# Index key, decay, beta and index weights in one tile of products, with the key rotated while the convolutions run

## The reference

```python
h = rms_norm(x, norm_g)
proj = jnp.einsum('btd,de->bte', h, w_in)
(qa, ka, va, za, ba, aa, ub, zb, qc, kc, vc, zc, iq, ik, iw, gates) = split_columns(proj)
# delta net: qa, ka, va through a convolution over 4 positions and silu; beta and decay per head
beta = jax.nn.sigmoid(ba)                       # 4 columns
g = -jnp.exp(a_log) * jax.nn.softplus(aa + dt_bias)   # 4 columns
# sparse attention: an indexer chooses the keys
qi = apply_rope(iq.reshape(b, t, 4, 64), cos_i, sin_i)
ki = apply_rope(ik.reshape(b, t, 1, 64), cos_i, sin_i)[:, :, 0]   # one key of 64 columns for 4 heads
wi = iw * (IDX_HEADS ** -0.5 * IDX_DIM ** -0.5)  # 4 columns
dots = jnp.einsum('bqhd,bsd->bqhs', qi_b, ki)
score = jnp.einsum('bqh,bqhs->bqs', wi_b, jax.nn.relu(dots))
_, idx = lax.top_k(score, topk)
```

## Time and profile before

| | |
|---|---|
| median of 3 runs | 1982.15 us (1980.84 to 1982.24) |
| the profiled execution, as timed | 1981.93 us |
| its span, first to last instruction | 1980.1 us |
| PE busy | 1967.1 us, 99% |
| DVE, ACT, POOL busy | 52%, 45%, 43% |
| granted TensorE clock | 1.00 over the span |

### The profile page before, as it was taken

One profiled execution on the slowest core, in us unless ns is written; L12 is line 12 of the kernel. 1 busy time (PEld: TensorE's weight loads), 2 busy tenths in 40 slices (PEclk: granted clock), 3 DMA queues, 4 the chain that ended last, 5 costly groups with the idle time before them and its releaser, 6 DMA issues.

```text
span 1980.1 us, 24451 instructions
## 1 busy us (share of the span) xinstructions
PE 1967.1 (99%) x9420; PEld 1561.4 (79%) x9420; DVE 1022.2 (52%) x1872; ACT 889.3 (45%) x1373; POOL 853.8 (43%) x646
## 2 busy tenths in 40 slices
PE   9999999999999999999999999999999999999999
PEld 6878878777788878787877788677777888888887
DVE  5657755555745568666365658476444346201210
ACT  6455553334345555543343355586455334322321
POOL 5545432433355444333434455455222455444443
PEclk9999999999999999999999999999999999999999
DMA  5334542423534235522424546322111322332332
GB/s 199 119 116 133 133 135 79 161 75 122 188 117 144 97 109 154 162 88 84 150 75 144 182 149 170 125 83 86 54 44 43 128 96 96 102 99 92 100 113 69
DMA packets 94995, 228.52 MB, mean 115 GB/s; under 512 B 29880, under 2 KB 32952, under 8 KB 93568
## 3 DMA queue, kind: packets, MB, share of 16 engines
q1 hardware_dynamic: 93408, 224.34, 35.6%
q10 hardware_dynamic: 1472, 2.62, 0.4%
HBM read 195.06 MB, written 24.64 MB: 111 GB/s over the span
## 4 chain that ended last, share of the span: by engine, by line
PE 85%; DVE 7%; ACT 2%; DMA 2%; SPq 1%; issue 1%; POOL 1%; ACTq 0%; DVEq 0%
PE bank L442 83%; PE bank L445 2%; SPq L371 1%; DVE ER L376 1%; DVE kv L376 1%; ACT lt L428 1%; DVE lt L386 1%; DVE scs L401 1%; DMA kv<-blocks 1%; DVE m8s L398 0%; DVE tmp L376 0%; POOL wl L376 0%; ACT L420 0%; DVE tmp L386 0%; ACT wh L431 0%
## 5 line engine op out<-in xcount | busy, mean ns | idle before, releaser
L376 POOL TENSOR_TENSOR wl<-st,wh 128x512 fp32r<-128x512 f32 x606 | 808.6, 1357 | 1049.3 <-ACT wh L431 1049.3
L442 PE MATMUL bank<-hh,wh 128*128 128x512 f32 x1632 | 658.9, 404 | 2.2 <-POOL hl L376 0.7
L442 PE MATMUL bank<-hh,wl 128*128 128x512 f32 x1632 | 636.1, 390 | 0.0
L442 PE MATMUL bank<-hl,wh 128*128 128x512 f32 x1632 | 635.6, 390 | 0.0
L431 ACT ACTIVATE wh<-st 128x1024 fp32r<-128x1024 f32 (+1 forms) x304 | 318.8, 1049 | 235.5 <-PE bank L442 188.3
L442 PEld LDWEIGHTS bank<-hh,wh 128*128 128x128 f32 x1632 | 306.4, 188 | 93.3 <-issue 25.8
L442 PEld LDWEIGHTS bank<-hl,wh 128*128 128x128 f32 x1632 | 306.6, 188 | 67.4 <-issue 6.9
L442 PEld LDWEIGHTS bank<-hh,wl 128*128 128x128 f32 x1632 | 306.3, 188 | 65.4
L376 DVE TENSOR_TENSOR xt<-xt,bank 128x512 f32<-128x512 f32 x40 | 27.4, 686 | 235.6 <-PE bank L442 235.6
L428 ACT ACTIVATE tmp<-bank 128x512 f32<-128x512 f32 x70 | 41.7, 596 | 157.7 <-PE bank L442 151.0
L442 PE MATMUL bank<-fh,wh 128*128 128x512 f32 x256 | 99.6, 389 | 0.0
(11 more groups left out here) (340 smaller groups left out, 2907.8 us busy)
## 6 DMA issues: line engine op xcount, KB each, us to landing
st<-units SPq DMA_DIRECT2D x302, 512.0 KB, 3.5
gates<-tmp SPq DMA_DIRECT2D x48, 256.0 KB, 2.8
gt<-gates SPq DMA_DIRECT2D x48, 256.0 KB, 3.7
pad<-tmp SPq DMA_DIRECT2D x32, 128.0 KB, 2.7
qk<-tmp SPq DMA_DIRECT2D x16, 256.0 KB, 4.3
x_scratch<-xt SPq DMA_DIRECT2D x2, 2048.0 KB, 8.7
xt<-x_scratch SPq DMA_DIRECT2D x2, 2048.0 KB, 8.4
ph<-phi SPq DMA_DIRECT2D x8, 512.0 KB, 4.7
```

Of the source, the lines that this page charges most:

```text
L376: return NOTHING if self.e is None else self.e.tensor_tensor(out, a, b, op)
L442: return NOTHING if self.e is None else self.e.matmul(out, lhsT, rhs, start=start, stop=stop, skip_group_check=share)
```

## The change

The 64 columns of the index key move into the unit of "small", at rows 64 to 127; the index weights move to rows 4 to 7. The tile ("ik") and its unit go, in both layers. ACT copies rows 64 to 127 of bank 4 out beside convolution 0; SP waits for that copy (after feeding two more units, and in layer 0 the load of the tables) and issues five DMAs: four make the swapped halves for both halves of the partitions, one doubles the key itself. DVE rotates it (three instructions) beside convolution 5. The index weights are written by DVE to rows 64 to 71 of `L.rw` (eight rows, of which 68 to 71 are used). ACT's gates 4 and 5 wait for the last convolution in place of `ki`. `proj` has 30 tiles for 31 on every engine; `delta`, `select` and their rates stay. The diff, cut to its core:

```diff
@@ plan, pack_units
-        out += [("p", l, 5128), ("p", l, 5256), ("ik", l)]
+        out += [("p", l, 5128), ("p", l, 5256)]
...
-            for c0, at in ((2048, 0), (2052, 32), (5448, 64)):
-                u[:, :, at:at + 4] = kmajor(w[:, c0:c0 + 4]).reshape(128, 8, 4)
+            for c0, at, m in ((2048, 0, 4), (5448, 4, 4), (2052, 32, 4), (5384, 64, 64)):
+                u[:, :, at:at + m] = kmajor(w[:, c0:c0 + m]).reshape(128, 8, m)
@@ build
+        L.ik, L.iks = [L.lT[:, c, :, :].rearrange("p a b -> p (a b)") for c in range(2)]
@@ tensor_program, proj
-                yield tile(("ik", l), 2, ("ik", l), g), idle(1)
@@ scalar_program, front1 and proj
                     ac.wait_ge(*done("small", l))
+                    ac.cp(L.ik[64:128, :], banks[4][64:128, :]).then_inc(*sig("ik", l))
...
-            def index_k():
-                ac.wait_ge(*done("ik", l))
-                ac.cp(tmp[2][:], banks[2][:]).then_inc(*sig("free2", "ik", l))
-                yield
...
-                ac.wait_ge(*(at("ki", l) if j < 6 else at(f"spill{gate_at(j)}", "gate", l, j - 2)))
+                ac.wait_ge(*(at("conv_v", l, 11, 4) if j < 6 else at(f"spill{gate_at(j)}", "gate", l, j - 2)))
...
-                yield tile(("ik", l)), index_k()
@@ vector_program, front1, proj and delta
-                    dv.ts(L.rw[R2, :], banks[4][R2, :], 1.0 / 16.0, ALU.mult).then_inc(*sig("free4", "small", l))
+                    dv.ts(L.rw[64:72, :], banks[4][0:8, :], 1.0 / 16.0, ALU.mult).then_inc(*sig("free4", "small", l))
+                if c == 5:
+                    dv.wait_ge(*at("tab", "A"))
+                    index(L.ki[:], L.ik, L.iks, at("swapik", l, 4), "ki", l)
...
-            def index_k():
-                yield
-                index(L.ki[:], tmp[2], tmp[3][:], at("swap2", l, 96), "ki", l)
...
-                yield idle(1), index_k()
...
-            dv.cp(L.wi[:], bv[:, :, 64:68]).then_inc(*sig("free4", "tp", l))
+            dv.cp(L.wi[:], bv[:, :, 68:72]).then_inc(*sig("free4", "tp", l))
@@ pool_program
-                for _ in range(31):
+                for _ in range(30):
@@ sync_program, proj and the layer's main line
-            def index_k():
-                sp.wait_ge(*at("free2", "ik", l))
-                swap(tmp[3], tmp[2], 32, "swap2", l)
-                yield
...
-                yield tile(), index_k()
...
             take(2)
             if l == 0:
                 sp.dma(tabs[:, 0:apack.n], tabA).then_inc(*dma("tab", "A"))
+
+            sp.wait_ge(*at("ik", l))
+            for f in range(2):
+                sp.dma(L.iks[64 * f:64 * f + 32, :], L.ik[96:128, :]).then_inc(*dma("swapik", l, 2 * f))
+                sp.dma(L.iks[64 * f + 32:64 * f + 64, :], L.ik[64:96, :]).then_inc(*dma("swapik", l, 2 * f + 1))
+            sp.dma(L.ik[0:64, :], L.ik[64:128, :]).then_inc(*dma("swapik", l, 4))
             take(10)
```

More of the change, by code:

```diff
@@ L2010, in rope, with index @@
             dv.tt(out, out, s1, ALU.add).then_inc(*sig(name, *key))
+        def index(out, x, xs, swapped, name, *key):
+            dv.wait_ge(*swapped)
+            dv.tt(out, x[:], TA("cosI"), ALU.mult).then_inc(*sig("rope", name, *key, 0))
+            dv.tt(xs, xs, TA("sinI"), ALU.mult).then_inc(*sig("rope", name, *key, 1))
+            dv.wait_ge(*at("rope", name, *key, 1))
+            dv.tt(out, out, xs, ALU.add).then_inc(*sig(name, *key))
         def front1(l):
@@ L2049, in proj @@
             dv.wait_ge(*at("tab", "A"))
[L2051 to L2056, removed]
             def index_q(c):
```

## The result

The changed kernel takes **1994.9 us** (median of 6 runs, 1992.9 to 2004.9) beside 1982.1 for the kernel before: ratio 1.0072, 95% interval 1.0051 to 1.0092. It is slower by 13 us; 1973.0 was forecast, so it missed the forecast by 22.

What follows compares the result with a forecast made beforehand. PE's work was taken to bound the kernel, DVE's inversion a close second limit. Layer 0: -5.44 - 0.9 + 1.4 - 1.3 + 1.2 = -5.0; layer 1: -4.0; together -9.1 from 1981.93, forecast 1973.0 us, range 1969.0 to 1977.5.

Steps and rivals of the forecast that it cites:

- A tile's worth: One tile of `proj` removed per layer saves PE 5.44 us, 10.9 us over two layers.
- 1, front1 at nothing: In front1, ACT's copy, DVE's 2.0 us rotation and SP's five DMAs fit into slack and cost nothing.
- 2, spreading for k: Start of `delta`: row 0's mean is computed while PE would wait for DVE's scaling of q; gain 0.9 us a layer.
- 3, row 1: Among the decay matrices: row 1's root ahead of head 1's decay delays head 1's products; loss 1.4 us a layer.
- 4, the inversion: Row 2's DVE work leaves the inversion, ending near 230; 2.4 us margin, `XT0` waits of 1.3 and 0.3 us go.
- The slower rival: Inversion comes late through waits in SP's list; slower from about 7 us lateness, 1988 at 10 us; chance 0.02.
- 5, the scan: End of `proj`: two more pieces of the scan stand bare; loss 1.2 us a layer (0.5 to 2).

Runs made afterwards that it cites:

- experiment 2: Changed kernel with gate 4 ahead of row 0, so every row stands against `delta` as in the kernel before: 1979.5 us.
- experiment 5: Kernel of experiment 2 with DVE's rotation of the second index query moved behind the scaling of q: 1971.1 us; the same edit on the kernel before: 1979.0.
- Experiment 1: Changed kernel plus a filler tile, read by nobody, in the index key tile's old place in `proj`: 1983.3 us, ratio 0.9998 to the kernel before.
- experiments 2 and 3, second kernel: The second kernel of 3: changed kernel with rows 1 to 5 alone one tile later, rows 0, 6 and 7 as changed: 1991.4 us.
- experiment 8: Changed kernel with GpSimd's splits of eleven units a layer shortened to 16 of 1024 columns, leaving part of the products out: 1973.4 us.
- experiment 7: Kernel of experiment 5 with PE made to wait ahead of convolution tile 6 for six ScalarE copies (1983.2 us) or two (1974.5 us).

## Why the prediction was wrong

**A tile's worth, right.** 5.4 us a layer less 0.9 for the scan: experiment 2's layer 0, experiment 5.

**1, front1 at nothing: right.** Experiment 1. The five DMAs took SP until 56.3 us, 1.6 later than worked out, and the next load went out 1.8 us later than before; the three units loaded ahead covered it. One of the rotation's multiplies took 1.79 us beside GpSimd's split; that was caught up too.

**2, spreading for k: right in layer 0 only.** 1.91 us there, as worked out. In layer 1 spreading took 2.75 us even behind row 0's mean, with a half clock after it (granted 0.57 from 712.93 to 716.93 us): the 0.9 was not had. The step took the wait for something that another instruction could fill; it was DVE's list in the wrong order, worth 1.7 us a layer in either kernel.

**3, row 1: right in the sum, high in the wait.** Head 1's products started at 157.21 (156.4 by the working), 0.6 of it brought along from before `proj`; PE stood 0.85 us for them, not 1.4. By head 3 the rows stand level again: its products started at 169.92, 168.92 before, so gain 2 and loss 3 together cost 0.4 without the 0.6, and the working has 0.5.

**4, the inversion: the step that failed.** The blocks (176.8 for 176), the start (186.70 for 186.4) and row 2's four instructions ahead of it came as worked out. The 4.7 us that they took inside it were taken off its length at an unchanged price for the rest. But GpSimd's splits go on at PE's pace, two of 1.3 us for each tile, and an instruction of DVE that reads two tensors from SBUF, running beside one, is held for up to its length: in the changed kernel's layer 0, 16 of the 62 instructions overlapped a split and took 1.05 us in the mean, the other 46 took 0.31, and `select`'s one-input MAX8, issued between them, kept its 0.42 to 0.43 us beside a split. With row 2 gone from their path the splits fell on the inversion, 11 instructions over 1 us for 8, 3.05 us more in sum (30.90 for 27.85), and on row 3, whose four took 1.26, 1.77, 1.00 and 1.66, 2.0 us more than before: together the 5 us that were to be won. Where row 2 is back inside (experiments 2 and 3, second kernel), the 62 take 27.84 and 27.85 again, and the inversion lasts 49.4 and 48.9 us: about the same with row 2 and without. So the inversion ended at 235.5, not 230: the 2.4 us of margin were gone. The working had the effect in a row, the 1.77 us multiply of the earlier trace rows, and used it as part of row 2's price, not as the split's. The Trainium skill's rule (GPSIMD Engine Reference, Specifications: contention with DVE instructions that have two SBUF inputs) agrees with 1.05 against 0.31, and with 0.36 for the 11 that overlapped the shortened splits; it was weighed for the rotation in front1, where there was slack, and not for the inversion, where there was none.

**What was left out: row 6.** The working followed the rows at the start of `delta` and up to the inversion, and stopped there; it named four places where the order changed. The fifth, row 6 against the heads, is where a late inversion is paid. It was put at nothing by not being named: without the splits it costs nothing, with the inversion 5.5 us later than worked out it costs 9.9 us in layer 0 (front3's first tile at 345.57, in experiment 8 at 335.66): 4.35 up to head 0's first product (0.46 of it from before `proj`), 3.88 more up to head 1's kt, and 1.68 behind it, where the half clock is. The slower rival had the right mechanism (the inversion late through SP's list) with the wrong cause, and its price was too low: it let the lateness cost its length beyond 2.4 us, which for the 5.5 us measured gives 1979, though each wait brings a second one through SP's list and the clock, and it got 0.02.

**5, the scan: right**, 0.9 for the 1.2 worked out, with the two waits of 0.78 us per layer.

Open: which length of stall brings the half clock; how the 5 us of lateness divide among the waits, since experiment 8 takes away 14; and how much of layer 1's larger loss is chance, since the changed kernel's two profiled executions differ by 3.2 us at its front3.

## What to carry to other kernels

Taking a tile out of a hand-woven order moves everything behind it against everything that is placed by count; follow every moved item to the end of the list, or fill the hole with an item that the other chains don't wait for, as gate 4 does, and keep the old relation. Where GpSimd works at a fixed pace beside VectorE, the price of a VectorE chain of two-input instructions is its own time plus a toll per GpSimd instruction, and removing work from the chain doesn't remove the toll. Look for an engine that waits for a queued transfer while work that is ready stands behind it, as the scaling of q did: one more step of delay for the waiting item gave 3 to 8 us, where the removal of two tiles gave 8.

## What was not expected of the hardware

The inversion's two-input VectorE instructions take 0.31 us in the mean alone and 1.05 beside a GpSimd split (0.36 beside shortened ones). A TensorE stall of 4.0 us cost 6.1 (experiment 7), one of 1.4 cost 1.7, which is within the noise of its length. Thirteen microseconds, 0.7% of a kernel whose TensorE shows 99% busy before and after, hung on waits of 2 to 5 us.
